# Sliding-window attention: keys in score order, a held rotation on GpSimd, and a moved gate projection

## The reference, cut to what matters

```python
for gi, (window, dilation) in enumerate(SWA_GROUPS):   # (128, 1), (512, 4), (2048, 16)
    o_g, lse_g = dilated_window_attention(q[:, :, gi], k_sh[:, :, gi], v_sh[:, :, gi], window, dilation)
    ...
wts = jax.nn.softmax(jnp.stack(lses, axis=0), axis=0)
o = jnp.sum(wts[..., None] * jnp.stack(outs, axis=0), axis=0)
o = o.reshape(bsz, s, SWA_OUT)
return (o.astype(x.dtype) * jax.nn.silu(g)) @ w_out
```

## Time and profile before

| | us |
|---|---|
| median of 3 runs | 3263.24 (3263.18 to 3263.65) |
| profiled execution, its own time | 3263.35 |
| its span, first to last instruction | 3261.5 |
| PE busy | 2843.2 (87%) |
| DVE busy | 1586.3 (49%) |
| ACT busy | 1120.1 (34%) |
| POOL busy | 1021.5 (31%) |

### The profile page before, as it was taken

One profiled execution on the slowest core, in us unless ns is written; L12 is line 12 of the kernel. 1 busy time (PEld: TensorE's weight loads), 2 busy tenths in 40 slices (PEclk: granted clock), 3 DMA queues, 4 the chain that ended last, 5 costly groups with the idle time before them and its releaser, 6 DMA issues. The chain is left out here.

```text
span 3261.5 us, 39814 instructions
## 1 busy us (share of the span) xinstructions
PE 2843.2 (87%) x14912; PEld 2352.9 (72%) x14912; DVE 1586.3 (49%) x1750; ACT 1120.1 (34%) x1789; POOL 1021.5 (31%) x520
## 2 busy tenths in 40 slices
PE   6988988599999999979189999999696979989887
PEld 5776776487888878868167777777574757878775
DVE  5453466804555155548835656566532134434344
ACT  3222222313333133341425555555512234434331
POOL 3453351256444464413033333333031330000001
PEclk9999998899999999989699999999897989999998
DMA  3010104322111121106111111111112110000021
GB/s 117 27 32 19 32 33 174 132 86 66 44 44 46 55 59 46 46 27 244 65 47 40 39 40 40 40 33 39 49 55 78 39 45 14 7 13 6 6 71 64
DMA packets 52940, 176.07 MB, mean 54 GB/s; under 512 B 8800, under 2 KB 10464, under 8 KB 52832
## 3 DMA queue, kind: packets, MB, share of 16 engines
q1 hardware_dynamic: 45920, 149.38, 14.6%
q10 hardware_dynamic: 6912, 25.17, 2.2%
HBM read 133.46 MB, written 16.94 MB: 46 GB/s over the span
## 5 line engine op out<-in xcount | busy, mean ns | idle before, releaser
L108 POOL TENSOR_SCALAR w_hi<-w_raw 128x1024 fp32r<-128x1024 f32 x156 | 174.2, 1117 | 2004.7 <-PE pj L134 696.0
L132 PE MATMUL pj<-x_hi,w_hi 128*128 128x512 f32 x1132 | 453.8, 401 | 63.4 <-PEq L580 24.6
L133 PE MATMUL pj<-x_lo,w_hi 128*128 128x512 f32 x1132 | 445.9, 394 | 0.0
L134 PE MATMUL pj<-x_hi,w_lo 128*128 128x512 f32 x1132 | 445.4, 393 | 0.0
L110 POOL TENSOR_TENSOR w_lo<-w_raw,w_hi 128x1024 fp32r<-128x1024 f32 x156 | 387.8, 2486 | 23.3 <-issue 9.9
L1049 PE MATMUL pj<-x_hi,w_hi 128*128 128x512 f32 x704 | 300.4, 427 | 34.5 <-PEq L580 34.5
L132 PEld LDWEIGHTS pj<-x_hi,w_hi 128*128 128x128 f32 x1132 | 216.3, 191 | 113.6 <-issue 65.4
L1050 PE MATMUL pj<-x_lo,w_hi 128*128 128x512 f32 x704 | 282.2, 401 | 0.0
L1051 PE MATMUL pj<-x_hi,w_lo 128*128 128x512 f32 x704 | 282.0, 401 | 0.0
L1458 PE MATMUL pj<-x_hi,w_hi 128*128 128x512 f32 x512 | 223.7, 437 | 33.9 <-DVEq L1665 26.2
L133 PEld LDWEIGHTS pj<-x_lo,w_hi 128*128 128x128 f32 x1132 | 216.1, 191 | 45.1 <-issue 1.7
(11 more groups left out here) (331 smaller groups left out, 5701.4 us busy)
## 6 DMA issues: line engine op xcount, KB each, us to landing
w_raw<-w_slots SPq DMA_DIRECT2D x158, 512.0 KB, 3.5
out_ada_rows<-ada_t ACTq DMA_DIRECT2D x48, 512.0 KB, 4.9
x_res<-o_t SPq DMA_DIRECT2D x12, 1024.0 KB, 4.0
swa_swapped<-swa_q SPq DMA_DIRECT2D x48, 256.0 KB, 3.6
o_t<-x_res SPq DMA_DIRECT2D x12, 1024.0 KB, 6.6
o_t<-x_t SPq DMA_DIRECT2D x8, 1024.0 KB, 10.9
da_swapped<-da_raw SPq DMA_DIRECT2D x64, 128.0 KB, 2.3
out_t<-o_t SPq DMA_DIRECT2D x4, 1024.0 KB, 4.4
```

What stands on the lines that cost most here:

```text
L108: nc.gpsimd.tensor_scalar(g.w_hi[:, u, :], g.w_raw[:, u, :], 1.0, 0.0, ALU.mult, ALU.add)
L132: nc.tensor.matmul(dst, w_hi, x_hi[:, k, cols], start=(j == 0), stop=False)
L133: nc.tensor.matmul(dst, w_hi, x_lo[:, k, cols], start=False, stop=False)
L134: mm = nc.tensor.matmul(dst, w_lo, x_hi[:, k, cols], start=False, stop=(j == n - 1))
```

## The change

Five edits. (1) All projected keys go to the query buffer first; POOL's last rotation instruction, for keys, reads with the group's stride and writes the keys in score order, without a stride. (2) Score matmuls read the keys without a stride, 256 columns at once in groups 0 and 1 (a first tile, which has none before it, still takes two of 128); odd and even tiles of group 1 now read alike, and the mask covers the rest. (3) POOL waits for `total_ready`, the end of the joining (L1319), before it splits slot z+3 and rotates; SP and ACT waits follow the new buffers. (4) `FIRST_T` is 13 in place of 14. (5) In the very last head the gate's eight pieces leave the score steps: four stand ahead of L1137, four ahead of L1140, and ACT's and DVE's gate steps move into the joining.

```diff
-        GAP, FIRST_T, COVER, FILL = 10, 14, 25, 27
+        GAP, FIRST_T, COVER, FILL = 10, 13, 25, 27
@@ sync, alone and head
-                        swap(keys if kind == "k" else qs, j, nz, rope_index(kind, j, kv), kind == "q" or j == 2)
+                        swap(qs, j, nz, rope_index(kind, j, kv), kind == "q" or j == 2)
@@ gpsimd, rope
-                nc.gpsimd.tensor_tensor(dst[:, j, :], dst[:, j, :], swp[:, j % 2, :], ALU.add).then_inc(m.rope_ready, 1)
+                if kind == "q":
+                    dst, a, b = qs[:, j, :], qs[:, j, :], swp[:, j % 2, :]
+                else:
+                    d = SWA_STRIDE[j]
+                    dst = keys[:, j, :].rearrange("p (r i) -> p r i", r=d)
+                    a, b = (x.rearrange("p (i r) -> p r i", r=d) for x in (qs[:, j, :], swp[:, j % 2, :]))
+                nc.gpsimd.tensor_tensor(dst, a, b, ALU.add).then_inc(m.rope_ready, 1)
@@ gpsimd, head
                     for j in range(G):
+                        if j == 0:
+                            pool.wait_ge(m.total_ready, h + 1)
                         split_slot(nc, pool, g, s0 + z + 3 + j, hh * 4)
@@ tensor, scores
-                        own = residue_tile(keys[:, gr, :], d, t)
-                        if w == P:
-                            mm = nc.tensor.matmul(bank(i % 2)[:, j * w:(j + 1) * w], q, own, start=True, stop=True)
+                        if t == 0 and w == 2 * P:
+                            nc.tensor.matmul(bank(i % 2)[:, 0:P], q, keys[:, gr, 0:P], start=True, stop=True)
+                            mm = nc.tensor.matmul(bank(i % 2)[:, P:2 * P], q, keys[:, gr, 0:P], start=True, stop=True)
                         else:
-                            before = residue_tile(keys[:, gr, :], d, t - 1) if len(swa_keys(gr, t)) == 2 else own
-                            nc.tensor.matmul(bank(i % 2)[:, j * w:j * w + P], q, before, start=True, stop=True)
-                            mm = nc.tensor.matmul(bank(i % 2)[:, j * w + P:(j + 1) * w], q, own, start=True, stop=True)
+                            mm = nc.tensor.matmul(bank(i % 2)[:, j * w:(j + 1) * w], q, keys[:, gr, (t + 1) * P - w:(t + 1) * P],
+                                                  start=True, stop=True)
@@ tensor, head
                 for i in range(N):
                     scores(i)
-                    fill(i, i + 1)
-                fill(GAP, FIRST_T)
+                    if nxt:
+                        fill(i, i + 1)
+                fill(*((GAP, FIRST_T) if nxt else (0, 4)))
                 pe.wait_ge(m.lse_ready, h + 1)
...
-                fill(FIRST_T, COVER)
+                fill(*((FIRST_T, COVER) if nxt else (4, 8)))
                 pe.wait_ge(m.total_in, h * 48 + 48)
@@ scalar, alone
-                            dst = (keys if kind == "k" else qs)[:, j, cols[half]]
+                            if kind == "q" and half == 0:
+                                act.wait_ge(m.rope_ready, kv * ROPES + (j + 1))
+                            dst = qs[:, j, cols[half]]
@@ scalar, head
                 take(0, 0)
+                if not nxt:
+                    gate(0)
                 act.wait_ge(m.lt_done, h + 1)
...
                 nc.scalar.activation(ee[:, :, :], ee[:, :, :], ACT.Exp).then_inc(m.terms_exp, 1)
+                if not nxt:
+                    gate(1)
```

More of the change, by code:

```diff
@@ L991, in head @@
                 if nxt:
-                    swap(qs if nxt == "q" else keys, 0, nz, rope, False, False)
+                    swap(qs, 0, nz, rope, False, False)
                 sp.wait_ge(m.total_ready, h + 1)
@@ L1004, in head @@
                     for j in (1, 2):
-                        swap(qs if nxt == "q" else keys, j, nz + j, rope + j, False, False)
+                        swap(qs, j, nz + j, rope + j, False, False)
                         load(z + (1 + j), (1 + j + 1) % 2)
@@ L1011, in _, with rope @@
         def _(pool):
-            def rope(dst, j, index, count):
+            def rope(kind, j, index, count):
                 pool.wait_ge(swapped[j % 2], count * 32 + 32)
                 nc.gpsimd.tensor_tensor(swp[:, j % 2, :], swp[:, j % 2, :], sin[:, :], ALU.mult)
-                nc.gpsimd.tensor_tensor(dst[:, j, :], dst[:, j, :], cos[:, :], ALU.mult)
+                nc.gpsimd.tensor_tensor(qs[:, j, :], qs[:, j, :], cos[:, :], ALU.mult)
                 pool.drain()
-                nc.gpsimd.tensor_tensor(dst[:, j, :], dst[:, j, :], swp[:, j % 2, :], ALU.add).then_inc(m.rope_ready, 1)
+                if kind == "q":
[5 more added lines that the diff above has]
+                nc.gpsimd.tensor_tensor(dst, a, b, ALU.add).then_inc(m.rope_ready, 1)
             def alone(kv):
@@ L1022, in alone @@
                     if kind != "v":
-                        rope(keys if kind == "k" else qs, j, rope_index(kind, j, kv), swap_count(kind, j, kv))
+                        rope(kind, j, rope_index(kind, j, kv), swap_count(kind, j, kv))
             def head(kv, hh, h, nxt):
@@ L1029, in head @@
                     for j in range(G):
+                        if j == 0:
+                            pool.wait_ge(m.total_ready, h + 1)
                         split_slot(nc, pool, g, s0 + z + 3 + j, hh * 4)
                         count = hh * 2 + (kv * 10 + 4 + j // 2) if j % 2 == 0 else hh + (kv * 5 + 2)
-                        rope(qs if nxt == "q" else keys, j, hh * G + (kv * ROPES + 2 * G + j), count)
+                        rope(nxt, j, hh * G + (kv * ROPES + 2 * G + j), count)
             pool.wait_ge(m.tables, 80)
@@ L1133, in head @@
                     scores(i)
-                    fill(i, i + 1)
-                fill(GAP, FIRST_T)
+                    if nxt:
+                        fill(i, i + 1)
+                fill(*((GAP, FIRST_T) if nxt else (0, 4)))
                 pe.wait_ge(m.lse_ready, h + 1)
                 nc.tensor.transpose(turn(0)[0:96, 0:P], lse[:, :], g.ident[:, :]).then_inc(m.lt_done, 1)
-                fill(FIRST_T, COVER)
+                fill(*((FIRST_T, COVER) if nxt else (4, 8)))
                 pe.wait_ge(m.total_in, h * 48 + 48)
                 nc.tensor.transpose(turn(1)[:, 0:96], back[0:96, :], g.ident[0:96, 0:96]).then_inc(m.bt_done, 1)
-                fill(COVER, FILL)
+                if nxt:
+                    fill(COVER, FILL)
                 for i in range(N + 1):
@@ L1144, in head @@
                         turn_p(i)
-                    fill(FILL + i, FILL + i + 1)
+                    if nxt:
+                        fill(FILL + i, FILL + i + 1)
                     if i >= 1:
@@ L1211, in take @@
                             act.wait_ge(m.rope_ready, hh * G + (kv * ROPES + 2 * G + j - (0 if j == 0 else 1)))
-                        evacuate((qs if nxt == "q" else keys)[:, j, cols[half]], z + (1 + j), nz + j, half)
+                        evacuate(qs[:, j, cols[half]], z + (1 + j), nz + j, half)
                 def take_p(i):
@@ L1221, in head @@
                     exp(i)
-                    if i in (4, 8):
+                    if nxt and i in (4, 8):
                         gate(i // 8)
@@ L1296, in head @@
                     shift(i)
-                    if i in (5, 9):
+                    if nxt and i in (5, 9):
                         gate(i // 9)
```

## The result

| | us |
|---|---|
| before, median of 4 runs | 3263.21 (3258.38 to 3263.65) |
| after, median of 4 runs | 3221.34 (3219.25 to 3223.74) |
| ratio, 95% interval | 0.9875 (0.9858 to 0.9892) |
| profiled execution of after, span | 3223.74, 3221.9 |
| its PE, DVE, ACT, POOL busy | 2815.3, 1603.6, 1122.0, 1042.0 |

The change makes the kernel 41.9 us faster (1.3%): the predicted sign, under half of the predicted 87 us, and above the range's end of 3214.

A forecast was written before the change was run, and what follows sets the result against it. PE was taken to wait for joined log-sums, slowed by POOL's work beside DVE's joining. Per head 6.5 + 2.3 - 0.9 + 3.85 + 1.0 = 12.75 us, times seven 89.3, less 2 for the last head: 3176 us, range 3153 to 3214.

The forecast's parts named there:

- rival D: Log-sum joining: the hold does nothing because DVE's joining was slow of itself; 3253 us, chance 0.03.
- rival A: Joined sums' way back stays late behind SP's load, L1140 2.5 us later and the clock falls; 3210 us, chance 0.22.
- The wait at L1149: PE's wait for joined sums falls from 6.8 to about 0.3 us a head, and 2.3 of low clock goes too.
- Keys, group 1: Score steps of group 1: each falls from 1.86 to 0.9 us, 3.85 us a head gained.
- Keys, group 2: Score steps of group 2: PE gains 1.9 us, of which 1.0 a head is kept; ends 0 and 1.9.
- so the stream costs: Score matmuls: the strided streamed keys, not the strided query weights, make them slow, judged by the value transposes.
- Rival C: Group 1 scores: the stride of 4 was free and the steps slow for another reason; 3203 us, chance 0.04.
- Normalization: Blocks beside POOL's postponed work: 0.9 us a head charged against the change, later blocks at about PE's pace of 2.7.
- The bound of 10: Normalization's worst case: all ten blocks behind POOL take 28 us where PE wants the last after 19.
- rival E: Held work lands wholly on normalization, PE waiting 10.4 us, and joining isn't shorter; slower at 3304 us, chance 0.03.
- The strided rotation: POOL's keys' rotation: between 2.39 us and twice that an instruction, covered by splits made a slot ahead; costs nothing.
- Last head: L1137 comes 8.5 us earlier, but log-sums wait behind SP's load of the split slot; 2 us against the change.

The follow-up runs named there:

- keys_only: The kernel before with only the keys' new order: POOL not held, FIRST_T 14, last head as before; 3235.31 us, ratio 0.9918.
- a_q_plain: The kernel after with query tiles read without a stride, so neither score operand is strided (output differs); 3208.44 us, one execution.
- b_q_plain: The kernel before with query tiles read without a stride, keys still strided (output differs); 3264.61 us, one execution.
- rotation_behind: After, with POOL waiting for all normalized blocks before rotation 0, SP's load behind the joined sums, last head's load and split delayed; 3169.32 us, ratio 0.9716.
- second_hold: The kernel after, with POOL also waiting for the last normalized block before split z+4; 3191.17 us, ratio 0.9777.
- hold_only: The kernel before with only POOL's wait for the totals added, FIRST_T 14; 3240.74 us, ratio 0.993.
- last_load: The kernel after with the last head's load(z, 1) put behind the transfers of log-sums and joined sums; 3213.59 us, ratio 0.9845.
- load_behind: The kernel after with SP's load of slot z+1 moved behind the way back of the joined sums; 3232.9 us, ratio 0.9903.

## Why the prediction was right or wrong

- **Bound and mechanism: right.** The joining is slow because of POOL and fast everywhere with the hold: L1325 is at 374 ns in the median, and rival D falls. The way back stands behind the held split, as forecast, and rival A falls too: its transfers took 3.8 us to L1149 (877.17 to 880.99), 3.6 forecast.
- **The wait at L1149: 6.8 to 1.1, forecast 0.3.** The second stage gained 4.5 us for 5.3 forecast: against the sum's times the load left 0.4 late, the way back 0.6, and L1149 came 0.9 late. The clock stayed up behind this wait in all seven heads, so the 2.3 us were there.
- **Keys, group 1: right.** 3.85 forecast; group 1's four steps themselves gained 3.3 (12.99 to 9.71 us in the second head), and the whole first stage 3.6 in keys_only. The shortfall is mostly group 1's first step, whose first tile keeps two matmuls of 128 columns: with its piece it takes 2.8 us, the next ones 2.3.
- **Keys, group 2: wrong, and "so the stream costs" is the step that failed.** It was forecast at 1.0 and gave 0.1. The sentence was true of the stream, but the prediction put the whole doubling down to it and took the strided query to be free, by the value transposes. Their strided loads take at most 213 ns, those of the scores 0.31 to 0.34 us, and a score instruction of 128 columns starts every 0.11 us when nothing is strided, so the query's stride alone keeps it at 0.24. (The hold of about 1 us that POOL's split was to put on step 8's negated maximum was oversized too: 0.35 us for 0.17 in the trace of before. The wait forecast from it, 0.9, came at 0.8 in a_q_plain.) Rival C fell: with the keys alone at a stride of 4 (b_q_plain) group 1 is hardly faster than before, 0.23 us an instruction. The Trainium skill (SBUF — State Buffer, the note on cachelines in Door 1: The DMA port swizzle) lets fp32 stride by up to 4 elements for free. The scores disagree for both operands: at a stride of 4, 0.23 us with the keys alone strided, 0.23 with the queries alone (group 1's first step in after), and 0.11 with neither (the same step in a_q_plain).
- **Normalization: the step that failed most.** Charged 0.9 us a head, it cost about 4.5: the third stage lost 2.25 although the clock gave back 2.3 there. Of the 5.6 us a head that are missing from the forecast 12.75, 3.65 are in this stage. (rotation_behind says the same: 27.8 less 23.2 is 4.6.) PE's waits before L1118 are 3.4 of it in an ordinary head and 5.0 in the fourth. The prediction took PE's pace as one piece a block, 2.7 us. That holds while pieces stand between the blocks; behind piece 31 PE wants a block every 1.0 us (the rows of second_hold: 892.10, 893.10), while DVE gives one in 2.8. The bound of 10 stood in the text; the value was taken near its lower end. Of rival E it was true that the work lands there, not that it costs more than the hold gains.
- **The strided rotation: "nothing" was wrong in one head.** In the change it takes 4.3 and 4.1 us in the fourth head, 4.13 and 3.85 with DVE idle, against 2.40 without a stride. The cover argument was right for PE and the splits (keys_only: no loss); it didn't ask who runs beside it. A DVE block waited for it (4545 ns), and where PE already waits for blocks that counts: with the fall of the clock behind it the fourth head lost 4.5 us more than the others, nearly all of it (4.1) against hold_only's fourth head, where the rotations have no stride.
- **Last head: right in sign and mechanism, and close by some luck** (+2 forecast, +1.3 measured). The forecast's parts were -8.5 and +10.6; measured were -10.1 and +11.6, two misses that cancel. The maskings of its steps are 1.62 us apart, not 1.76. The price was SP's detour, as worked out: L985 left 10.0 us behind L1146, 9.6 forecast. What the forecast didn't see is that POOL's split stands behind the detour (last_load: 6.7 of the 11.6 come back, not all).

The sum with measured terms is 50.0 - 4.5 - 1.3 = 44 us in the SWA heads, against 87 forecast and 41.9 by the medians of whole executions.

Open: which share of the fourth head's 4.5 us is the clock's and which the wait for the rotation itself; second_hold removes both at once.

## What to carry to other kernels

Work moved off one contended stretch lands on the next one: before holding an engine back, list everything that the held engine does until it has caught up and who runs beside it, and take the consumer's pace there piece by piece, not its mean. Here the hold paid in full only with a second hold around the next contended stretch. Order matters too: a transfer made earlier lost 11.6 us, by falls of the clock, while the stretch behind it was contended, and gained 9 once it was free. And one trace of another kind of instruction does not price a stride: take each operand's stride away by itself.

## What the runs showed of the hardware

- While POOL works, DVE instructions with two inputs in SBUF go at about one per POOL instruction: 2833 ns in the median for 678, however short they are by themselves (L1332 in last_load: 2.38 us for 0.36). A small one with a single input was held up too (1.59 us for 0.17). POOL is slowed as well, L108 from 1.06 to 1.49 us.
- In the fp32 score matmuls of 128 columns a stride of 4 or 8 elements in either operand doubles the time of an instruction, from 0.11 to 0.23 or 0.24 us; two strides cost no more than one; under 256 columns the strided weight load is nearly hidden (0.23 for 0.22). The value transposes, with the same strides in their weights, stay at 0.11 to 0.12.
- POOL's addition with both inputs strided took 4.13 us (stride 4) and 3.85 (stride 8) with DVE out of its way, 2.40 without a stride: 72 and 60% more. The Trainium skill (GPSIMD Engine Reference, Performance pitfalls for Q7 kernels) has about half as much again for a read with an element step over 8 bytes; the direction agrees, the size here, with two such reads, is larger.
- One wait of 1.2 us behind full work left the granted clock at 1.00. Waits of 1.65 and 1.54 us, 4.2 us apart, came with a fall to 0.50, 1.2 GHz, for 6.8 us (fourth head, from 1052.7); the second head's 1.54 and 1.04 had none. In load_behind waits of 0.8, 1.5 and 1.4 us stand in the normalization of six heads; in three of them the clock fell and in three it did not.
